# A gated recurrence in which every group takes its three gate panels in front of its block gates

## The reference, cut to what matters

```python
def rglru_mixer(u, w_in, conv_w, conv_b, w_a, b_a, w_x, b_x, lam, w_out):
    proj = u @ w_in
    xr, g = jnp.split(proj, [R_WIDTH], axis=-1)          # R_WIDTH = 1536
    xc = causal_dwconv(xr, conv_w, conv_b)               # 4 taps along the tokens
    xb = xc.reshape(bsz, s, R_BLOCKS, R_BS)              # 8 blocks of 192
    r = jax.nn.sigmoid(jnp.einsum('bsnc,ncd->bsnd', xb, w_a).reshape(bsz, s, R_WIDTH) + b_a)
    ig = jax.nn.sigmoid(jnp.einsum('bsnc,ncd->bsnd', xb, w_x).reshape(bsz, s, R_WIDTH) + b_x)
    log_a = -LRU_C * r.astype(jnp.float32) * jax.nn.softplus(-lam.astype(jnp.float32))
    a = jnp.exp(log_a)
    bt = jnp.sqrt(-jnp.expm1(2.0 * log_a)) * (ig * xc).astype(jnp.float32)
    hs = linear_scan(a, bt).astype(u.dtype)              # h = a_t h + b_t
    y = hs * jax.nn.silu(g)
    return y @ w_out
```

## Time and profile before

| | us |
|---|---|
| median of 3 runs | 1672.15 |
| lowest and highest | 1671.86, 1672.67 |
| profiled execution | 1669.99 |
| its span | 1668.0 |
| PE busy | 1635.0 (98%) |
| DVE busy | 840.9 (50%) |
| ACT busy | 819.1 (49%) |

### The profile page before, as it was taken

The page is one execution under the profiler, slowest core; times in us unless marked ns, Lnnn a source line. Parts: engine busy times, 40 slices in busy tenths (PEclk is TensorE's granted clock), DMA queues, the critical chain, the costliest instruction groups (busy, mean ns, idle before and its releaser), DMA issues.

```text
span 1668.0 us, 21466 instructions
## 1 busy us (share of the span) xinstructions
PE 1635.0 (98%) x7637; PEld 1339.5 (80%) x7637; DVE 840.9 (50%) x1265; ACT 819.1 (49%) x1086; POOL 710.8 (43%) x933
## 2 busy tenths in 40 slices
PE   7999999999999999999999999999999999999997
PEld 6888888888888888888887878877877877788875
DVE  3566667631124212121255668258258258679676
ACT  6467776743334323142357545345345444654764
POOL 7353332356666555555574646445535631000000
PEclk9999999999999999999999999999999999999999
DMA  6231221123333333333332322322412313232311
GB/s 205 77 89 55 61 73 57 58 67 110 94 108 101 89 101 98 92 100 101 90 99 76 78 65 81 106 64 65 125 51 76 114 39 94 87 91 75 101 57 60
DMA packets 251095, 142.94 MB, mean 86 GB/s; under 512 B 6161, under 2 KB 249618, under 8 KB 251026
## 3 DMA queue, kind: packets, MB, share of 16 engines
q1 hardware_dynamic: 251026, 142.00, 29.3%
HBM read 139.89 MB, written 2.10 MB: 85 GB/s over the span
## 4 chain that ended last, share of the span: by engine, by line
PE 73%; DVE 5%; ACT 1%; issue 0%; DVEq 0%; ACTq 0%
PE bank L786 19%; PE bank L787 19%; PE bank L792 19%; PE bank L1127 2%; PE bank L777 2%; PE bank L779 2%; PE bank L778 2%; PE bank L1106 1%; PE bank L1091 1%; PE bank L1090 1%; PE bank L1089 1%; DVE xT L2100 1%; DVE w_lo L2377 1%; PE bank L1217 1%; PE bank L1218 1%; PE bank L1219 1%
## 5 line engine op out<-in xcount | busy, mean ns | idle before, releaser
L757 POOL TENSOR_TENSOR w_lo<-raw,w_hi 128x256 fp32r<-128x256 f32 x896 | 700.4, 814 | 674.9 <-ACT w_hi L1305 674.8
L1305 ACT ACTIVATE w_hi<-raw 128x1024 fp32r<-128x1024 f32 x264 | 277.5, 1056 | 531.4 <-PE bank L792 474.6
L786 PE MATMUL bank<-h_hi,w_hi 128*128 128x512 f32 x1252 | 497.5, 397 | 0.0
L787 PE MATMUL bank<-h_lo,w_hi 128*128 128x512 f32 x1252 | 487.9, 390 | 0.0
L792 PE MATMUL bank<-h_hi,w_lo 128*128 128x512 f32 x1252 | 309.3, 389 | 0.0
L786 PEld LDWEIGHTS bank<-h_hi,w_hi 128*128 128x128 f32 x1252 | 235.0, 188 | 55.7 <-issue 7.5
L787 PEld LDWEIGHTS bank<-h_lo,w_hi 128*128 128x128 f32 x1252 | 235.1, 188 | 52.3 <-issue 4.3
L792 PEld LDWEIGHTS bank<-h_hi,w_lo 128*128 128x128 f32 x1252 | 235.0, 188 | 48.8
L2100 DVE TENSOR_TENSOR xT<-xT,bank 128x512 f32<-128x512 f32 x103 | 68.2, 685 | 208.2 <-PE bank L792 156.9
L2125 DVE SCALAR_TENSOR_TENSOR fr<-bank,rstd 128x512 f32<-128x512 f32 x32 | 22.1, 692 | 133.6 <-PE bank L792 128.0
L786 PE MATMUL bank<-f_hi,w_hi 128*128 128x512 f32 x224 | 87.1, 389 | 0.0
(11 more groups left out here) (410 smaller groups left out, 2680.2 us busy)
## 6 DMA issues: line engine op xcount, KB each, us to landing
raw<-in_w_ff SPq DMA_DIRECT2D x64, 512.0 KB, 4.0
raw<-in_w_in SPq DMA_DIRECT2D x56, 512.0 KB, 3.7
raw<-in_m_w_in SPq DMA_DIRECT2D x48, 512.0 KB, 3.9
raw<-in_r_w_in SPq DMA_DIRECT2D x24, 512.0 KB, 3.7
raw<-in_m_w_out SPq DMA_DIRECT2D x16, 512.0 KB, 3.3
raw<-in_r_w_out SPq DMA_DIRECT2D x16, 384.0 KB, 3.1
raw<-in_w_up_b SPq DMA_DIRECT2D x8, 512.0 KB, 4.1
raw<-in_w_out SPq DMA_DIRECT2D x8, 512.0 KB, 4.1
```

Of the source, the lines that this page charges most:

```text
L757: ins = pool.tensor_tensor(w_lo[:, s, part], raw[:, s, part], w_hi[:, s, part].bitcast(F32), ALU.subtract)
L786: pe.matmul(dst, w_hi[:, s, c], hi[:, k, :], start=(k == 0), stop=False)
L787: pe.matmul(dst, w_hi[:, s, c], lo[:, k, :], start=False, stop=False)
L1305: act.activation(w_hi[:, p % RING, :], raw[:, p % RING, :], ACT.Copy).then_inc(hi_ready[p % RING], 1)
```

## The change

`r_order` gives x, 0, 1, 2, a for groups 0 and 3 as well. DVE's `r_gate(i, 2)` and ACT's `r_silu(i, 2)` stand in front of the block gates in all groups.

```diff
@@ r_order
     if i == 0:
-        return ["x", 0, 1, "a", 2]
+        return ["x", 0, 1, 2, "a"]
     if i < RG - 1:
         return ["x", 0, 1, 2, "a", ("o", i - 1)]
-    return ["x", 0, 1, "a", 2, ("o", i - 1), ("o", i)]
+    return ["x", 0, 1, 2, "a", ("o", i - 1), ("o", i)]
@@ ACT
                 r_silu(i, 0)
                 r_silu(i, 1)
-                if 0 < i < RG - 1:
-                    r_silu(i, 2)
+                r_silu(i, 2)
                 r_gates(i)
                 if i + 1 < RG:
                     r_gate_split(i + 1)
                 if i == RG - 1:
-                    r_silu(i, 2)
                     for c in range(RT):
                         r_y(i, c)
                         follow(R_OP[i - 1] + c)
@@
                     r_y(i, 1)
-                    if i == 0:
-                        r_silu(i, 2)
@@ DVE
                 out = 0 < i < RG - 1
-                if out:
-                    r_gate(i, 2)
+                r_gate(i, 2)
                 for c in range(RT):
                     if out:
                         r_add(i - 1, 2 * c)
                         r_add(i - 1, 2 * c + 1)
                     r_root(i, c)
-                if not out:
-                    r_gate(i, 2)
                 r_scan(i, 0)
```

## The result

| | us |
|---|---|
| before, median of 10 runs (lowest, highest) | 1671.96 (1668.91, 1672.96) |
| changed kernel, median of 10 runs (lowest, highest) | 1675.57 (1673.99, 1678.47) |
| ratio, 95% interval | 1.0026, 1.0018 to 1.0034 |
| profiled execution after, its span | 1674.49, 1672.7 |

The account below looks back on a forecast made before the run. PE is busy 98% of the span, but DVE's scans and sums set the end. 2.50 + 1.91 + 1.1 = 5.5 us takes the profiled 1669.99 to 1675.5, plus 2.2 gives 1677.6; range 1672.6 to 1680.0.

Parts of the forecast that it names:

- Group 0: DVE's first scan 2.00 us later, group 1's first sigmoid 3.21 later, so group 0's outputs start 2.50 later.
- Group 3: Last mixer's group 3: first scan and end 1.91 us later; the PE's saved 1.6 us counts for nothing.
- The clock: Granted clock may fall after the PE's idle time ahead of group 1's a4: 0 to 1.7 us, put at 1.1.
- The cover in group 2's outputs: Third output panel waits 3.9 us; a clock fall there costs nothing, with about 6 us to spare.
- Rival A: Last mixer: only the PE's gaps count, saving 1.95 us in group 0 and 1.6 in group 3: 1668.6; chance 0.10.
- B: Group 0: some of DVE's lateness is absorbed, only group 3 costs: 1672.1 to 1674.1, centre 1672.8; chance 0.13.
- C: Clock falls in groups 1 and 3, group 3's outputs come behind their banks: 7.8 us, 1680.0; chance 0.11.
- The table load: Ahead of group 1's first SiLU on ACT: 1.30 us from load start to SiLU, not 2.66 with a drain.

Follow-up runs that it names:

- group 0 alone: The kernel before with the new order (g2 ahead of the block gates) in group 0 only: 1673.44 against 1670.48, ratio 1.0014.
- before with both: The kernel before plus a one-column Sqrt on ACT and three DVE multiplications in group 0, PE order unchanged: group 0's outputs start 4.40 us later.
- group 3 alone: The kernel before with the new order (g2 ahead of the block gates) in group 3 only: 1671.92 against 1670.48, ratio 1.0013.
- run on POOL: The kernel before with the lower halves of the last six weight panels made by POOL, not DVE: 1673.47 against 1670.48, ratio 1.0015.
- early table: The changed kernel plus a one-column SiLU in group 0, loading the table in ACT's idle time: 1675.14 against 1670.48, ratio 1.0020.
- table again: The kernel before plus a one-column Sqrt on ACT behind group 0's last SiLU, forcing a SiLU table reload: group 0's outputs start 0.65 us later.

## Why the prediction was right

- **Direction and mechanism.** Slower, by two terms that have nothing to do with the PE's two gaps. Both terms were found apart and add up (2.72 + 2.01 against 4.69), where 2.50 + 1.91 = 4.41 was forecast.
- **Group 0.** DVE's first scan was forecast 2.00 later. It is 2.07 (1463.02 less the mixer's 0.10, against 1460.85), and g0's scaling in group 1 is 2.08. The first sigmoid was put 3.21 later and came 3.25. The missing 0.2 in the term lie at the last wait: a4 starts 2.57 later (1498.10 - 1411.76 against 1495.43 - 1411.66) where 2.50 was forecast, and the 15 matmuls behind it take 3.54 us (1501.64 - 1498.10) and not 3.40, as the first matmuls after a wait start up to 0.34 us apart instead of 0.23. The waits inside group 1's gates come to 4.65 us (1501.64 - 1487.47 less 9.52) against 4.4.
- **Group 3.** 1.91 forecast, 2.01 measured. That the PE's 1.6 us would count for nothing holds: the gap in front of a0 has become the 3.85 us ahead of the third output panel (3.9 forecast).
- **The clock** is the term that was mis-sized. Its 1.1 us were a mean over 0 and 1.7, and the profiled execution had 0: the fall came in one of three profiled executions with the wait of 2.15 us (the changed kernel, group 0 alone, and before with both), and cost 1.6 when it came. So the trace has 4.7 and the forecast 5.5, and the cluster means, 4.6 and 4.9, leave little for the clock too. Without this term the forecast would have been 4.4, and 0.3 short of the trace for the reasons above; the two errors go opposite ways, and that 1677.6 lies only 2.0 over the measured median owes something to that.
- **The cover in group 2's outputs** was stated wrongly. I gave the third panel 6 us to spare. What covers it are the two waits of before, 1.17 and 1.78 us, with the new starts behind them, 3.3 us in all. The fall used 1.6 of it in the changed kernel, where the third panel takes 5.68 us (1630.77 to 1636.45) instead of 4.09 and 1.71 of waiting are left, and 2.7 with group 3 alone, where 0.64 are left. That is also more than the 1.7 that I had as the most a fall costs. The cost was nothing, as forecast, but by a margin of 0.64 us.
- **Rival A** had the busy share of 98% for it and fell on the second landmark; **B** fell with group 0 alone; **C** (7.8 us) needed two falls that both count, and none was seen to cost in the tail.
- **The table load** was taken from the row (1.30 behind its start) and not with the drain: 1.41 between neighbours with and without it, and +0.65 for it alone where 1.9 was expected with the drain, settle that.

## What to carry to other kernels

A gap of the bottleneck engine can be filled and nothing won, if what it does later waits for an engine that the new order has made late: follow the work moved through every engine's list up to the next place where the bottleneck waits, and compare the lateness with the slack there (here 0.7 us for 3.2). Where a function table stays loaded across two uses, moving the first use moves the load in front of the second, perhaps out of idle time onto the path. For gains below the spread of runs, compare landmarks in two traces from the last common point, and read the granted clock between them: one fall was worth 1.6 us of the 4.40 above.

## What the runs showed of the hardware that was not expected

The times of the kernel before spread from 1669.41 to 1673.23 in 33 runs, in two clusters. In the ten profiled executions of this case, which run the same program up to the mixer, such a spread arises ahead of it: the mixer starts between 1410.95 and 1411.76 in six and between 1413.42 and 1414.52 in four. Between the execution of before and the one with group 0 alone it starts 2.47 us apart. The first PE instructions take 6.53 us in the latter (first line) and 5.50 in before (second line):

```profile
8.42 6.53 PE L829 MATMUL bank<-ident,xtok 128*128 128x128 f32 x32 [8.42 <-DMA xtok<-in_x]
```

```profile
8.53 5.50 PE L829 MATMUL bank<-ident,xtok 128*128 128x128 f32 x32 [8.53 <-DMA xtok<-in_x]
```

so that they end 0.92 us later, and one stretch of the mLSTM stage runs at half clock in it (first line, group 0 alone) and not in the other (second line, before):

```profile
1148.00:1151.00 3.00, 3.00 (x9) 2.33 (x8) 2.89 (x4) 1.48 (x3) 1.97 (x3) 0.52 0.00 0
```

```profile
1147.00:1150.00 3.00, 3.00 (x15) 2.47 (x14) 2.86 (x5) 1.60 (x3) 1.84 (x2) 1.00 0.00 0
```

The PE shows no wait ahead of that fall. The run on POOL has a fall at the same place; the two others of the four late ones (early table, table again) have one at 1274 to 1282 instead (0.74 to 0.83), and none where the other eight have it, behind the wait of 1.92 us at 1383.77. Below are the 3.6 us behind that wait in before (first line) and with the early table (second line):

```profile
1383.77:1387.37 3.60, 3.51 (x9) 2.36 (x10) 3.33 (x4) 1.59 (x3) 2.57 (x4) 0.59 0.10 29
```

```profile
1385.76:1389.36 3.60, 2.79 (x11) 2.04 (x12) 3.33 (x4) 1.59 (x3) 2.56 (x4) 1.00 0.10 30
```

So whether a clock fall follows one and the same wait differs between executions: after 1.92 us it came in eight of ten, after 2.15 us in one of three. The wait of 1.71 to 1.80 us ahead of group 3's outputs was never followed by one in eight executions, nor was one of 2.76 us there in the run on POOL, while one of 1.77 us at 1390.61 of the changed kernel was. After the 3.85 us it came in all three profiled executions that have it (changed, group 3 alone, early table). How long a wait has to be is left open.
